# Two transformer blocks on one core: attention walked by blocks of queries, with the output product of the first 512 tokens beside it

## The reference

```python
xn = rmsnorm(x, norm_mix_g)
u, g_lru, q, k, v, z = split(xn @ w_in)          # q: 16 heads of 64, k and v: 4 heads of 64
y_a = (h_fwd + h_bwd) * gelu(g_lru)              # conv of u, block-diagonal gates, two scans over the tokens
# attention: blocks of 128 queries, each sees the block before, itself and the block after
scores = einsum(q * 64**-0.5, k) + alibi         # |distance| <= 128, else -1e30
m = maximum(max(scores), sink)
p = exp(scores - m)
y_b = einsum(p / (sum(p) + exp(sink - m)), v)
gates = sigmoid(z + b_gate)
x = x + (gates[0] * y_a + gates[1] * y_b) @ w_out
xn2 = rmsnorm(x, norm_ffn_g)
x = x + (silu(xn2 @ w_gate) * (xn2 @ w_up)) @ w_ffn_out
return rmsnorm(x, norm_final_g)
```

## Time and profile before

| | |
|---|---|
| three runs | 3584.53, 3585.77, 3589.38 us; median 3585.77 |
| the profiled execution | 3588.67 us, its span 3587.3 us |
| PE busy | 3424.1 us (95%) |
| DVE, ACT, POOL busy | 1679.0, 1195.3, 276.0 us |
| mean granted PE clock | 0.983 of 2.4 GHz |
| HBM read, written | 274.99, 84.41 MB |

### The profile page before, as it was taken

How to read it: one execution, slowest core, us unless ns; L and a number is a source line. 1 busy time by engine, 2 the same in 40 slices (tenths; PEclk the granted TensorE clock), 3 DMA queues, 4 the chain that set the end, 5 groups by cost and what they waited for, 6 DMA issues and landing times.

```text
span 3587.3 us, 38750 instructions
## 1 busy us (share of the span) xinstructions
PE 3424.1 (95%) x15342; PEld 2769.9 (77%) x15342; DVE 1679.0 (47%) x2475; ACT 1195.3 (33%) x1936; POOL 276.0 (8%) x384
## 2 busy tenths in 40 slices
PE   6999999999999999999998999999978999999998
PEld 3788888877788788888886788886646788888886
DVE  4573434454334433433435466657685433333334
ACT  3592222234332311111113366655564311111112
POOL 0121000011100100000001110011111100000002
PEclk9999999999999999999998999999999999999999
DMA  5365433354542111111111434335333111111111
GB/s 204 117 213 183 143 118 121 118 188 163 189 141 94 59 59 47 47 47 47 47 48 36 156 132 141 132 118 145 104 91 124 59 59 48 47 47 47 47 47 59
DMA packets 171987, 361.94 MB, mean 101 GB/s; under 512 B 20512, under 2 KB 82592, under 8 KB 170528
## 3 DMA queue, kind: packets, MB, share of 16 engines
q1 hardware_dynamic: 147296, 279.23, 24.5%
q0 software_dynamic: 24512, 80.24, 5.9%
HBM read 274.99 MB, written 84.41 MB: 100 GB/s over the span
## 4 chain that ended last, share of the span: by engine, by line
PE 85%; DVE 7%; DMA 3%; ACT 2%; issue 2%; POOL 1%; SPq 0%; DVEq 0%; ACTq 0%; POOLq 0%
PE p L277 21%; PE p L279 21%; PE p L278 21%; PE p L1892 4%; PE p L1893 4%; PE p L1894 4%; PE p L2605 1%; PE p L1122 1%; PE p L1112 1%; PE p L1113 1%; DVE s_wl L238 1%; PE p L2592 1%; PE p L539 1%; DMA s_ad<-i_ada 1%; DMA s_aw<-i_adaT 1%
## 5 line engine op out<-in xcount | busy, mean ns | idle before, releaser
L277 PE MATMUL p<-s_xh,s_wh 128*128 128x512 f32 x3536 | 1401.7, 396 | 28.4 <-ACT s_xh L1510 10.4
L279 PE MATMUL p<-s_xh,s_wl 128*128 128x512 f32 x3536 | 1381.8, 391 | 0.0
L278 PE MATMUL p<-s_xl,s_wh 128*128 128x512 f32 x3536 | 1381.5, 391 | 0.0
L277 PEld LDWEIGHTS p<-s_xh,s_wh 128*128 128x128 f32 x3536 | 667.8, 189 | 174.5 <-ACT s_xh L1510 13.6
L278 PEld LDWEIGHTS p<-s_xl,s_wh 128*128 128x128 f32 x3536 | 667.5, 189 | 141.3 <-issue 4.9
L279 PEld LDWEIGHTS p<-s_xh,s_wl 128*128 128x128 f32 x3536 | 666.7, 189 | 140.6
L238 DVE TENSOR_TENSOR s_wl<-s_ws,s_wh 128x1024 fp32r<-128x1024 f32 x265 | 325.0, 1253 | 207.2 <-ACT s_wh L230 206.9
L230 ACT ACTIVATE s_wh<-s_ws 128x1024 fp32r<-128x1024 f32 x265 | 269.5, 1048 | 408.6 <-PE p L1894 357.7
L1940 DVE TENSOR_TENSOR s_tmp<-p,s_tmp 128x512 f32<-128x512 f32 x88 | 60.9, 692 | 663.0 <-ACT s_tmp L1916 335.7
L1916 ACT ACTIVATE s_tmp<-p 128x512 f32<-128x512 f32 x88 | 52.6, 598 | 692.8 <-PE p L279 692.8
L1892 PE MATMUL p<-s_fh,s_wh 128*128 128x512 f32 x704 | 280.2, 398 | 0.0
(11 more groups left out here) (283 smaller groups left out, 3100.1 us busy)
## 6 DMA issues: line engine op xcount, KB each, us to landing
s_ws<-i_Wf SPq DMA_DIRECT2D x132, 512.0 KB, 4.1
s_aw<-i_adaT SPq DMA_DIRECT2D x32, 512.0 KB, 3.7
s_gv<-d_v SPq DMA_DIRECT2D x20, 512.0 KB, 4.6
s_ad<-i_ada SPq DMA_DIRECT2D x8, 1024.0 KB, 6.6
s_ws<-i_Wu SPq DMA_DIRECT2D x16, 512.0 KB, 3.7
d_u<-s_tmp POOLq DMA_DIRECT2D x32, 256.0 KB, 3.5
s_ws<-i_Wwo SPq DMA_DIRECT2D x16, 512.0 KB, 4.7
s_ws<-i_Wz SPq DMA_DIRECT2D x16, 512.0 KB, 4.3
```

Source lines behind the costliest of these rows:

```text
L277: pe.matmul(o, wh, H[:, k, c:c + n], start=(k == 0), stop=False)
L278: pe.matmul(o, wh, L[:, k, c:c + n], start=False, stop=False)
L279: last = pe.matmul(o, wl, H[:, k, c:c + n], start=False, stop=(k == 7))
```

## The change

What it does, in the order of the program:

- The order of weight tiles has all eight q2 tiles in stage 5; z1 and wo2 are each walked twice, once per half (`z1b` and `wo2b` are the same weights loaded a second time), so 16 more tiles are loaded and split.
- Stage 5 has 74 jobs: all of q2, and z1 for the first half of the tokens. The LRU steps are spread evenly over them (61 steps on 74 jobs in place of one per job). k2 and q2 jobs are of a new kind `split`: ACT copies the high part to one slot, DVE makes the low part from the bank to a second slot (`low_part`), and the bank is free only behind DVE. DVE does this at the head of the next job's step. Both parts are stored.
- Stage 6 walks blocks first, then head pairs, then key heads. q and k come in parts, ready to use, through POOL's DMA queue. DVE no longer divides: it builds a diagonal of 0.5/denominator for four heads in one instruction (`inverse_dve`), and PE's turn is a full matmul of the weights with that diagonal. The values are weighed once per pair of units, in 64-column groups: key head 0 writes partitions 0 to 63 of bank 7, key head 1 partitions 64 to 127. Gate, merge and split of y are done in place by DVE and ACT; the round trip of y through DRAM is gone. The 16 jobs beside it are z1 for the second half (8), then wo2 for the first half (8), whose result goes to DRAM; their places are listed in `places`.
- `stage7` takes the place of residual_stage("wo2"): 8 jobs for the second half; beside them the stored first half is loaded, the residual added, squares summed, and the norm of the first half made between the jobs.

```diff
@@ weight_order
-    order += [("q2", m) for m in range(4)] + [("z1", m) for m in range(4)]
-    order += [("q2", m) for m in range(4, 8)] + [("z1", m) for m in range(4, 8)]
-    order += [("wo2", m) for m in range(8)]
+    order += [("q2", m) for m in range(8)] + [("z1", m) for m in range(8)]
+    order += [("z1b", m) for m in range(8)] + [("wo2", m) for m in range(8)] + [("wo2b", m) for m in range(8)]
@@ plan_fill, fill_act, fill_dve, fill_pool
-                frees(p, "A")
+                frees(p, "D" if kind == "split" else "A")
...
+        if p.kind == "split":
+            ac.activation(o.bitcast(R), ps, ACT.Copy, scale=p.scale).then_inc(*split_hi.up())
...
+    def low_part(p):
+        DVW.wait_ge(*p.hi)
+        for t in p.slot2_free:
+            DVW.wait_ge(*t)
+        dv.scalar_tensor_tensor(out=TMP[:, p.slot2, 0:p.n].bitcast(R), in0=B[p.bank][:, 0:p.n], scalar=p.scale, in1=TMP[:, p.slot, 0:p.n],
+                                op0=ALU.mult, op1=ALU.subtract).then_inc(*evD.up())
...
         if p.starts:
             weights_dve(ahead(p.i, 1))
+        if p.split_before:
+            low_part(p.split_before)
...
+            po.dma_start(q.dst[0][q.m][:, c], TMP[:, q.slot, 0:q.n].bitcast(R)).then_inc(*stored[q.slot].up())
+            POW.wait_ge(*q.ev)
+            po.dma_start(q.dst[1][q.m][:, c], TMP[:, q.slot2, 0:q.n].bitcast(R)).then_inc(*stored[q.slot2].up())
@@ stage5
-        steps = beside(len(jobs), [("lru", w) for w in work], 1)
+        steps = beside(len(jobs), [("lru", w) for w in work], len(work) / len(jobs))
@@ stage6
-        units = [(pair, blk, kv) for pair in range(2) for blk in range(8) for kv in range(2)]
+        units = [(blk, pair, kv) for blk in range(8) for pair in range(2) for kv in range(2)]
...
-        steps = beside(len(jobs), [("unit", u) for u in range(n_units + 4)], 1, -1)
+        places = [-1, -1, 0, 1, 2, 4, 7, 10] + [20, 22, 25, 28, 31, 32, 33, 34]
...
+        def turn_pe(u):
+            PEW.wait_ge(*inverse.at(u + 1))
...
-                    x = pe.transpose(B[b][:, c * 128:c * 128 + 128], PR[u % 3][:, a, c * 128:c * 128 + 128], ident[:])
+                    x = pe.matmul(B[b][:, c * 128:c * 128 + 128], PR[u % 3][:, a, c * 128:c * 128 + 128], DG[u % 2][:, a, :], start=True, stop=True)
...
+        def weigh_pe(g):
+            PEW.wait_ge(*copied.at(8 * g + 8))
...
+            for c in range(n // 128):
+                for kv in range(2):
+                    f = 64 * (2 * pair + kv)
+                    x = pe.matmul(B[7][64 * kv:64 * kv + 64, :].rearrange("p (a t) -> p a t", a=4), Vt[:, k0 + c, f:f + 64], PT[kv][:, :, c, :],
+                                  start=(c == 0), stop=(c == n // 128 - 1))
...
-            for a in range(4):
-                dv.tensor_scalar(P[:, a, 0:n], P[:, a, 0:n], dn[:, a:a + 1], 0.5, ALU.mult, ALU.mult).then_inc(*divided.up())
+            DVW.wait_ge(*turned.at(4 * (u - 1)))
+            dv.scalar_tensor_tensor(out=DG[u % 2][:, :, :], in0=ident[:, :].rearrange("p (o t) -> p o t", o=1).to_broadcast([128, 4, 128]), scalar=0.5,
+                                    in1=dn[:, :].rearrange("p (c o) -> p c o", o=1).to_broadcast([128, 4, 128]), op0=ALU.mult, op1=ALU.mult).then_inc(*inverse.up())
+
+        def gate_dve(g):
...
+            dv.scalar_tensor_tensor(out=ZB[s], in0=ZB[s], scalar=1.0, in1=B[7][:, :].rearrange("p (a t) -> p a t", a=4), op0=ALU.add, op1=ALU.mult).then_inc(*gated.up())
...
+            dv.tensor_tensor(ZB[s], ZB[s], MB[s], ALU.add).then_inc(*merged.up())
...
+        def pool_():
+            for t in gone:
+                POW.wait_ge(*t)
+            for x in range(4):
...
+                for y in range(2):
+                    po.dma_start(K1[64 * y:64 * y + 64, x, :], dKh[x // 2][c, :]).then_inc(*key_in[x].up())
+                po.dma_start(K2[0:64, x, :], dKl[x // 2][c, :]).then_inc(*key_in[x].up())
+                if x < 2:
+                    q_load(x)
@@ stage7
+            for f in first:
+                residual_sp(f.q, f.free, f.m, 0)
...
+                sp.dma_start(RES[:, f.m, 0:512], dW2[f.m][:, 0:512]).then_inc(*part_in[f.m % 4].up())
...
+        def pe_():
+            products_pe(pairs[0])
+            products_pe(pairs[1], {4: lambda: sums_pe(s0)})
+            products_pe(pairs[2], {4: lambda: spread_pe(0, DIA[:, 0, :], s0.diag, n0.q[7])})
+            products_pe(pairs[3])
```

More of the change, by code:

```diff
@@ L215, in program @@
     tile_of = {nm: i for i, nm in enumerate(order)}
-    cols_of = [D["W" + name][m].shape[1] for name, m in order]
+    tiles = [D["W" + AGAIN.get(name, name)][m] for name, m in order]
+    cols_of = [t.shape[1] for t in tiles]
     used = {}
@@ L323, in plan_fill @@
                     p.turned_before = before
-                if kind == "turned":
+                p.split_before = before if before is not None and before.kind == "split" else None
+                if kind == "split":
+                    p.hi = split_hi.due()
+                    p.slot, p.slot_free = take_slot()
+                    store_planned(p.slot, (key, m))
+                    p.slot2, p.slot2_free = take_slot()
+                    store_planned(p.slot2, (key, m))
+                elif kind == "turned":
                     p.vq = turns % 4
@@ L2454, in stage6 @@
-        jobs = plan_fill(items, [0, 1], 2, parts, [])
-        x_free = jobs[-1].mm
-        todo = [(i, h) for i in range(4) for h in range(2)] + [(i, 0) for i in range(4, 8)] + [(i, 1) for i in range(4, 8)]
-        y_steps, raw = [[] for _ in range(n_units + 4)], []
-        for u in range(n_units + 3):
-            if raw:
-                y_steps[u].append(("split", raw.pop(0)))
-            if u >= 20 and (todo[0][0] < 4 or (u >= 27 and todo[0][1] == 0)):
-                y_steps[u].append(("load", todo[0]))
-                raw.append(todo.pop(0))
@@ new lines, in stage6 @@
+        gated, merged = sig("dv", "gated"), sig("dv", "merged")
+        y_x = [x_tokens(1)[0] for g in range(16)]
+        new = [[y_x[8 * h + 6 + k // 4] for k in range(8)] for h in range(2)]
+        ready = {"second": (TC + 512, 1, 512, (XH, XL), XT[1]), "new first": (TC, 0, 512, (XH, XL), new[0])}
+        items = [("z1b", m, "second", "tanh", dZ1, "z1b", 1.0, TC) for m in range(8)]
+        items += [("wo2", m, "new first", "plain", dW2, "wo2", 1.0, TC) for m in range(8)]
+        sc_free, turn_free, out_free = {b: bank_free[b] for b in (2, 3, 4)}, {b: bank_free[b] for b in (5, 6)}, bank_free[7]
@@ L2489, in span @@
+        jobs = plan_fill(items, [0, 1], 2, lambda which: [ready[which]], [])
+        x_free = [first_half_done, jobs[7].mm]
+        places = [-1, -1, 0, 1, 2, 4, 7, 10] + [20, 22, 25, 28, 31, 32, 33, 34]
+        steps = []
+        for u in range(-1, n_units + 4):
+            steps += ([("unit", u)] if u >= 0 else []) + [("fill", j) for j in range(16) if places[j] == u]
         def span(u):
-            blk = units[u][1]
+            blk = units[u][0]
             k0, k1 = max(0, blk - 1), min(8, blk + 2)
@@ L2699, in exps_dve @@
         def exps_dve(u):
-            pair, blk, kv = units[u]
+            blk, pair, kv = units[u]
             k0, n, a0 = span(u)
@@ L2782, in pool_ @@
                     fill_pool(jobs[u])
-                elif 3 <= u <= n_units + 2 and units[u - 3][2] == 1:
-                    weigh_pool(u - 3)
+                elif u + 2 < n_units:
+                    q_load(u + 2)
         pool_()
```

434 lines of the change are left out of this document (228 added, 206 removed).

## The result

| | before | after |
|---|---|---|
| median (range) of four runs on one chip, us | 3586.62 (3584.53 to 3589.38) | 3631.24 (3630.19 to 3634.84) |
| span of the profiled execution, us | 3587.3 | 3628.9 |
| PE busy, us | 3424.1 | 3443.0 |
| DVE, ACT, POOL busy, us | 1679.0, 1195.3, 276.0 | 1668.5, 1193.8, 303.5 |

The ratio is 1.0126, 95% interval [1.0108, 1.0143]: slower by 45 us, where 24 us faster was forecast; the time lies outside the range of 3546 to 3598.

The account below looks back on a forecast made before the run. PE bounds everything except the last 140 us of stage 6, where DVE does. Terms +43.7 + 11 - 36.7 - 43.7 + 1 = -24.7 us, applied to the median: 3562 us, 8-in-10 range 3546 to 3598.

Parts of the forecast that it names:

- +11 [in stage 5]: Stage 5: PE loses 11 us waiting for banks freed behind DVE's low part, range 0 to 20, besides +43.7 for added jobs.
- the pattern: Stage 5: long recurrence steps and a weight split delay DVE's low part, costing PE 5.5 us each time, expected twice.
- That puts the first scores at 15.4, so 4.5 of waiting: Stage 6 start: after two jobs (10.9 us), PE waits 4.5 us for merge, store and loads, in place of 5.4.
- Units 6 to 27: Mid stage 6: eleven pairs of units, six without a job at 13.3 us and five with one at 17.7, 168.3 together.
- A pair without a job is then DVE's, 13.3: Stage 6: DVE's work of 13.1 us, against PE's 12.0, sets a pair of units without a job at 13.3 us.
- Rival 1: Stage 6 weighing: the column groups run one after another, so PE sets the stage, +30 us; chance 0.30, centred on 3589.
- Rival 2: Stage 6: attention keeps its pace of 8.0 us a unit through the loop of PE, ACT and DVE, +38, 3600; chance 0.13.
- So +1 net [in stage 7]: Stage 7, beyond -43.7 for fewer jobs: old seam goes, new waits at column sums and feed-forward come; between -6 and +8.
- the seam of 7.7: Old wait between stage 6's jobs and the feed-forward, expected to go because the first half's norm is made between jobs.
- Rival 3: Stage 5 loses nothing because DVE meets the low parts on time: 3551 us; counted inside the likeliest case's 0.57.
- its moved jobs: Stage 5: eight jobs added, +43.7 us, with eight fewer in stage 7, -43.7.

Follow-up runs that it names:

- bankact: Changed kernel, but DVE makes the low parts from ACT's copy, so ACT alone frees the bank (low parts' values left out): 3594.09 us.
- Rate1: Changed kernel with one recurrence step after each stage 5 product, as before the change, instead of steps spread over all: 3610.36 us.
- bankrate: Changed kernel with three PSUM banks instead of two for stage 5's products and one recurrence step after each product: 3587.57 us.
- seam: Changed kernel, requesting half of the keys and the values at stage 6's start only once the first score is done: 3631.94 us.
- serial: Changed kernel with the weighted sums running all key blocks of one 64-column group, then the other, instead of alternating: 3639.97 us.

## Why the prediction was wrong

The forecast was -24.7 by the trace, measured +40.4 from the marker, 65.1 apart. By its own terms:

1. **"So I take +11 [in stage 5], with 0 as the low end ... and 20 as the high one": 41.5.** This step failed, and carries 30.5 of the 65. The mechanism was right (bankact removes it: 37 us at the first scores), its count and its price were not. I looked for the pattern in DVE's order alone and found it twice; there are six waits on a low part and one, of 4.0, for a turned v2 product. I set the high part at 1.5 us behind the job's end each time and kept ACT's lag for the high end of the range; ACT's "decay" step and weight split put it 6 to 7 us later. I expected the k2 and v2 jobs to be clear of the recurrence, and one wait stands at each. And I had no term for the slow clock behind a wait, 12.2 us in all. That DVE was idle a third of the time was no cover: an idle engine was waiting for the other one in the chain.
2. **"That puts the first scores at 15.4, so 4.5 of waiting": 27.3 and 16.2.** The merge ends 7.8 us after the last job, not 3.4, and the first key load leaves at 11.8, where the working has 7.4 (3.4 and 4). From there to the first scores it took 15.5 us, not 8.0: a load was priced by rows of a quiet time, and here sixteen leave POOL's queue within 12 us. Rate1 and bankrate settle the first half: with the recurrence done early the first key load leaves 2.2 us after the last job, and the wait is 7.8 and 4.6. The second half is only in part shown: in seam the queries' low part landed in 5.6 us where it took 6.9 to 10.5, but the time from the first key load to the first scores varied by 3.6 us in the same code.
3. **Stage 6 otherwise: 10 us over, spread thin.** Units 6 to 27 took 172.5 for 168.3 (four of the five pairs with a job 18.6 to 18.9 for 17.7), the end 59.9 for 55.5, the first six units 1.3 more. What lengthened the pairs with a job is not settled; in the one from 2613 PE waits 1.3 us for DVE's bias. **"A pair without a job is then DVE's, 13.3"** gave the right length by luck: DVE needs 12.5, not 13.1, and the rest is its wait of 0.86 for PE's scores. By serial each 0.9 us of PE's weighing is 0.9 of the pair. Rival 1 did not come about (the groups overlap). Rival 2's loop is there, though at 0.9 us a pair and not the 2.75 that it priced.
4. **"So +1 net [in stage 7]", with +8 as the upper bound: +13.8.** The chain to the column sums was right in kind (7 forecast, 11.4 measured): the first residual load left 6.6 us in, not 4. A wait of 2.3 for a weight split stands at the feed-forward, for the 1 to 2 forecast. Beside them are 4.9 us without a term: the ten matmuls of the column sums and the spread hold PE for 2.2, and the slow starts behind the wait of 11.4 and behind the spread are most of the rest (the granted clock is 0.89 in the stage). Before, such matmuls stood inside the seam of 7.7 that the working struck out whole. The wait within the feed-forward, 4.1, took the place of the 2.9 in the earlier trace rows.

So the loss came mostly from the three places that feed and drain attention's loop, and the loop itself, the part that I had examined most, has the forecast pace for a reason other than the one given. Rival 3 (stage 5 loses nothing) is what banks and rate together nearly give: 6.0 us of idle time there and first scores 15.6 us after stage 5, as forecast. Yet the time is 3587.6, not 3551, since stage 5 still has 6.9 us over its moved jobs, attention its 10 and stage 7 its 13 over the forecast.

## What to carry to other kernels

When an edit lets a second engine free a buffer that one engine freed, walk both engines' orders for every such release, and add their longest steps, before looking at how busy either is; if a spare buffer exists, give it to this ring first. Price a stage's first loads by how many go out with them, and find out which last step of the old stage gates them: spreading side work evenly to the very end puts its end on the path. A wait of a few microseconds on PE can cost a slower stretch behind it beside its length. When a stage comes out at the forecast pace, still look at what its bounding engine waits for: the number can be right for another reason.
